# Differential attention: score products of 32 fp32 rows replaced by one split pass over 128-row stacks

## The chip, the cores and the metric

The kernel runs on one core of one Trainium2 chip. The metric is the device time of one execution in microseconds (us). Engines are called PE (TensorE; PEld is its weight load), DVE (VectorE), ACT (ScalarE), POOL (GpSimd) and SP (SyncE, which issues most DMAs). They run their own instruction streams in order and wait for each other by semaphores.

## The reference, cut to what matters

A two-layer backbone over 512 latent tokens and 256 context tokens of width 1024. Each layer normalises the tokens, projects them, and runs four branches (retention, gated linear attention, grouped-query attention, differential attention), whose outputs are projected, gated and summed; then comes a gated MLP. Only differential attention is touched:

```python
def diff_branch(zl, zc, q_norm, k_norm, lam_vecs, subln, layer_idx, rope, need_ctx):
    ...
    ql, kl, vl = prep(zl, True)        # RMS norm of q and k per 32 channels, then rotary (latent tokens only)
    qc, kc, vc = prep(zc, False)
    scale = DIFF_DQK ** -0.5           # DIFF_DQK = 32, 4 heads, 2 maps each
    ...
    ol = blocked_attention(ql, jnp.concatenate([kl, kc], axis=2), jnp.concatenate([v_lat, v_lat], axis=1), scale)
    y_l = combine(ol)                  # o = map0 - lam * map1, then RMS norm
    y_c = combine(blocked_attention(qc, kc, ..., scale)) if need_ctx else None   # layer 0 only
```

So for each of 4 heads and each block of 128 queries there are two score maps, each a product over 32 channels, softmaxed apart and subtracted. Latent queries (4 blocks) see 768 keys, context queries (2 blocks, in layer 0 only) see 256.

## The kernel before, in words

Everything is transposed: channels on the 128 partitions, tokens along the row. All large products are split: an fp32 matrix is kept as a leading part (rounded to the type fp32r, which PE takes in one pass) and a rest (fp32 minus leading part), and a product is three fp32r products: leading x leading, leading x rest, rest x leading (`product`, lines 537 to 539; `token_part`, lines 581 to 583). The weights are split on the fly: SP loads 128x1024 tiles into a ring of four, POOL writes leading part (line 1354) and rest (line 1357) of one half tile after the other (`split`, `split_until`), and PE uses them. Two tiles of split halves fit. POOL therefore runs through the weight tiles in a fixed order, and in program order it does nothing else but the exponents of the gated branch and the rests of the merged sum.

In a layer the branches follow each other on PE. For differential attention the projection of four feature tiles of 128 channels comes first, in the order 2, 3 (keys of heads 0, 1 and of heads 2, 3), 0, 1 (queries of the same heads); then a token projection for the values; then the softmax with its products. Behind each feature tile come its mean squares and, one or two tiles later, the rotation of its channels by a permutation product (`rotate`), which DVE then finishes (`turn`, lines 2130 to 2133). The rotation of tile 0 stands behind the token projection, that of tile 1 behind the transposes of the grouped-query outputs (`turn_outputs`, line 995). The queries' roots don't scale the queries but the scores, by `query_scale`, later.

The outputs of the grouped branch, the first gate tile of the branch (`early_parts`) and then the softmax follow on PE. The softmax waits until the last query tile is rotated. It walks over pairs (query block t, head h), 24 in layer 0 and 16 in layer 1. In each step PE issues the score products of the next head (`scores`, line 827), a share of the gate projection (`among`: 8 gate tiles in layer 0, 10 in layer 1, spread over the steps), and then transposes and value products of the present head (lines 847 and 743). The score products of map 0 and map 1 lie in PSUM banks 0, 1 and 2, 3; each step uses the same banks, so it waits until ACT has taken the exponentials of the step before. DVE finds the maxima (lines 2215, 2216), ACT the exponentials (line 1679), DVE the difference of the maps (lines 2244 to 2246) and every fourth step the normalisation of a query block (lines 2224 to 2235).

A score product before is a plain fp32 product over 32 rows of the rotated tile:

```python
lo, n, qi, ki = 64 * (h % 2) + 32 * m, 32, h // 2, 2 + h // 2
mm = pe.matmul(psum(key)[:, x:y], q[lo:lo + n, qi, t * P:(t + 1) * P], q[lo:lo + n, ki, x:y], ...)
```

Of the kernel before, what the change touches and what calls it, by code (L numbers as in the profile page):

```python
# [245 lines left out]
def bass_hybrid_backbone(nc, A, out, marks):  # L246
# [6 lines left out]
    with ctx:  # L253
# [3 lines left out]
        xT = sb("xT", [P, KT, T])  # L257
        hh_at = nc.sbuf_base
        hh = sb("hh", [P, KT, T], F32R)
        hl = sb("hl", [P, KT, T], F32R)  # L260
# [6 lines left out]
        small = sb("small", [P, sum(w for _, w in SMALL)])  # L267
        rope = sb("rope", [P, 6, LAT])
        dist = sb("dist", [P, 7 * P])
        mask = sb("mask", [P, len(LEVELS), P], U8)  # L270
# [119 lines left out]
        prob = prob.rearrange("p (b m t) -> p b m t", b=2, m=2)  # L390
        pt_s = pt_s.rearrange("p (b t) -> p b t", b=2)

        G = {}
# [119 lines left out]
        def _(pe):  # L513
# [284 lines left out]
            def softmax(l, b):  # L798
# [16 lines left out]

                def scores(t, h):
                    for m in range(maps):
                        for s, c in room(("s", l, b, t, h, m), *((0, 1) if (m if b == "dif" else h % 2) == 0 else (2, 3))):
                            pe.wait_ge(s, c)
                    for x, y in (segs(T) if t < TL else [(LAT, T)]):  # L820
                        for m in range(maps):
                            key = ("s", l, b, t, h, m)
                            if b == "dif":
                                lo, n, qi, ki = 64 * (h % 2) + 32 * m, 32, h // 2, 2 + h // 2
                            else:
                                lo, n, qi, ki = 64 * (h % 2), 64, h // 2, 2 if h // 2 == h % 2 else 3
# [200 lines left out]
            for l in range(DEPTH):  # L1027
# [27 lines left out]
                for b in ORDER:  # L1055
                    nf, nt = len(BR[b]["feat"]), len(BR[b]["tok"])
                    lag = 4 if b == "ret" else 2
                    for j in range(nf + lag):
# [32 lines left out]
                        if b == "dif" and lag <= j < nf + lag - 1:  # L1091
                            rotate(l, b, feature_order(b)[j - lag])
# [232 lines left out]
        def _(pool):  # L1325
# [43 lines left out]
            def rest_of_sum(l, u):  # L1369
# [49 lines left out]
        def _(act):  # L1419
# [197 lines left out]
            def queries_out(l, b, n):  # L1617
# [7 lines left out]
                ins.then_inc(*up("queries", ("turnable", l, b, n)))  # L1625

            def features_out(l, n):

# [25 lines left out]
            def softmax(l, b):  # L1654
# [15 lines left out]
                for n, (t, h) in enumerate(order):  # L1670
# [3 lines left out]
                    for m in range(maps):  # L1674
# [5 lines left out]
                                       bias=nmx[:, c:c + 1],  # L1680
                                       accum_out=rsum[t % 2][:, 4 * m + h:4 * m + h + 1]).then_inc(*up("act_free", ("free", key)))
                    if b == "dif" and n >= 1:
                        transposed(n - 1)
# [193 lines left out]
        def _(dve):  # L1877
# [206 lines left out]
            def prep_tiles(l, b):  # L2084
# [55 lines left out]
                for n in keys if b == "dif" else ():  # L2140
                    if n != keys[0]:
                        turn(n - 1)
                    normalise(n)
                turn(keys[-1])
# [58 lines left out]
            def softmax(l, b):  # L2203
# [81 lines left out]
                for n in range(len(order)):  # L2285
                    t, h = order[n]
                    differ(n)
                    if n + 1 < len(order):
# [270 lines left out]
```

## Time and profile before

| | |
|---|---|
| time, median of 3 runs | 2677.52 us (2672.38 to 2679.13) |
| profiled execution, its own time | 2680.3 us |
| its span, first to last instruction | 2678.5 us |
| busy: PE, PEld, DVE, ACT, POOL | 2558.4, 2120.3, 1361.4, 761.3, 1483.1 us |
| mean granted TensorE clock | 0.986 |
| differential score products | from 708.5 us (layer 0) to 2167.4 us (layer 1) |

Times in the rows are microseconds from the start of the span, durations of single instructions in the views by line are nanoseconds. A row of the order of time gives start, duration, engine, line, operation, what it writes and reads, and in brackets the idle time of its engine before it and what ended that. A matmul's duration includes the way through the array; what PE spends on one is read from the distance of two starts. An fp32 matmul shows as two records, so eight records are the four products of one head.

### The profile page before, as it was taken

How to read it: one execution, taken by the hardware profiler on the slowest of the kernel's cores; microseconds unless marked ns; L12 is line 12 of the kernel's file. 1: busy time of each engine (PE TensorE's matmuls, PEld its weight loads, DVE VectorE, ACT ScalarE, POOL GpSimd, SP SyncE). 2: the span in 40 equal slices, each digit the busy share in tenths (PEclk: the TensorE clock that was granted, in tenths of full speed). 3: DMA queues.
4: the chain of work that ended last, by engine and by line, in shares of the span. 5: the costliest groups of instructions: out<-in, count | busy, mean ns of one | idle time of the engine just before them, and what ended most of it. 6: DMA issues, size and time to landing. Idle time of an engine off the chain costs nothing.

```text
span 2678.5 us, 37843 instructions
## 1 busy us (share of the span) xinstructions
PE 2558.4 (96%) x15408; PEld 2120.3 (79%) x15408; DVE 1361.4 (51%) x1877; ACT 761.3 (28%) x1276; POOL 1483.1 (55%) x1375
## 2 busy tenths in 40 slices
PE   5999999999999999999999999999998998999999
PEld 2788878877777888888878888797877777888777
DVE  3632157643577877555564462327754677521231
ACT  4611333432355511111120123133522454111200
POOL 2443457522423627666669436447834445688886
PEclk8999999999999999999999999999999999999999
DMA  7422312312213833444434462212321237333322
GB/s 270 150 74 95 111 56 70 91 45 93 78 51 98 272 110 111 125 121 117 125 102 118 125 216 77 60 48 79 79 60 48 71 122 220 114 100 95 95 85 81
DMA packets 378210, 285.10 MB, mean 106 GB/s; under 512 B 10309, under 2 KB 338729, under 8 KB 377526
## 3 DMA queue, kind: packets, MB, share of 16 engines
q1 hardware_dynamic: 375744, 279.81, 34.9%
q8 instruction: 123, 2.02, 0.3%
q10 hardware_dynamic: 1686, 2.78, 0.3%
q14 instruction: 49, 0.40, 0.0%
q0 software_dynamic: 608, 0.09, 0.0%
HBM read 253.28 MB, written 29.36 MB: 106 GB/s over the span
## 4 chain that ended last, share of the span: by engine, by line
PE 81%; DVE 9%; POOL 3%; ACT 3%; issue 2%; DMA 1%; ACTq 0%; DVEq 0%; SPq 0%; POOLq 0%
PE ps L537 18%; PE ps L538 17%; PE ps L539 17%; PE ps L1203 3%; PE ps L743 3%; PE ps L581 2%; PE ps L582 2%; PE ps L583 2%; PE ps L827 2%; DVE ffl L2485 2%; POOL w_lo L1357 2%; PE ps L847 2%; PE ps L1152 1%; POOL w_hi L1354 1%; PE ps L955 1%
## 5 line engine op out<-in xcount | busy, mean ns | idle before, releaser
L1354 POOL TENSOR_TENSOR w_hi<-ring,tiny 128x512 fp32r<-128x512 f32 x480 | 535.8, 1116 | 987.4 <-PE ps L539 581.8
L537 PE MATMUL ps<-hh,w_hi 128*128 128x512 f32 (+1 forms) x2320 | 844.4, 364 | 9.9 <-DVE hl L2039 9.0
L1357 POOL TENSOR_TENSOR w_lo<-ring,w_hi 128x512 fp32r<-128x512 f32 (+1 forms) x568 | 798.7, 1409 | 83.5 <-ACT w_hi L1560 45.8
L538 PE MATMUL ps<-hl,w_hi 128*128 128x512 f32 (+1 forms) x2320 | 820.8, 354 | 0.0
L539 PE MATMUL ps<-hh,w_lo 128*128 128x512 f32 (+1 forms) x2320 | 819.9, 353 | 0.0
L537 PEld LDWEIGHTS ps<-hh,w_hi 128*128 128x128 f32 x2320 | 443.1, 191 | 103.4 <-issue 27.1
L539 PEld LDWEIGHTS ps<-hh,w_lo 128*128 128x128 f32 x2320 | 442.9, 191 | 61.8
L538 PEld LDWEIGHTS ps<-hl,w_hi 128*128 128x128 f32 x2320 | 444.0, 191 | 56.1 <-issue 1.0
L1679 ACT ACTIVATE arena<-ps,tiny,vec 128x768 f32<-128x768 f32 (+1 forms) x120 | 108.7, 906 | 188.1 <-DVE tiny L2216 188.0
L1851 ACT ACTIVATE arena<-ps,vec 128x768 f32<-128x768 f32 (+1 forms) x44 | 39.1, 888 | 425.2 <-PE ps L539 425.2
L2494 DVE SCALAR_TENSOR_TENSOR arena<-ps,vec,arena 128x511 f32<-128x511 f32 x66 | 43.6, 661 | 221.3 <-ACT arena L1851 220.5
L537 PE MATMUL ps<-ffh,w_hi 128*128 128x512 f32 x352 | 139.7, 397 | 12.9 <-DVE ffl L2485 11.4
L1962 DVE SCALAR_TENSOR_TENSOR rope<-ring,tiny,rope 128x1024 f32<-128x1024 f32 x84 | 145.4, 1772 | 0.9
L581 PE MATMUL ps<-w_hi,hh 128*128 128x256 f32 x448 | 131.1, 293 | 7.5 <-ACT arena L1613 7.4
L539 PE MATMUL ps<-ffh,w_lo 128*128 128x512 f32 x352 | 137.1, 390 | 0.0
L538 PE MATMUL ps<-ffl,w_hi 128*128 128x512 f32 x352 | 137.1, 390 | 0.0
L582 PE MATMUL ps<-w_lo,hh 128*128 128x256 f32 x448 | 128.6, 287 | 0.0
L583 PE MATMUL ps<-w_hi,hl 128*128 128x256 f32 x448 | 128.5, 287 | 0.0
L2215 DVE TENSOR_REDUCE tiny<-ps 128x1 f32<-128x768 f32 (+1 forms) x120 | 101.3, 845 | 52.7 <-PE ps L811 34.2
L1540 ACT ACTIVATE arena<-ps 128x512 f32<-128x512 f32 (+3 forms) x108 | 59.5, 551 | 192.1 <-PE ps L539 189.7
L581 PEld LDWEIGHTS ps<-w_hi,hh 128*128 128x128 f32 x448 | 88.0, 196 | 13.8 <-ACT arena L1613 8.5
L537 PEld LDWEIGHTS ps<-ffh,w_hi 128*128 128x128 f32 x352 | 66.0, 188 | 36.9 <-DVE ffl L2485 15.8
(271 smaller groups left out, 3820.9 us busy)
## 6 DMA issues: line engine op xcount, KB each, us to landing
ring<-in_w_in SPq DMA_DIRECT2D x118, 512.0 KB, 4.0
ring<-in_w_mod SPq DMA_DIRECT2D x96, 512.0 KB, 3.9
ring<-in_w_up SPq DMA_DIRECT2D x88, 512.0 KB, 4.2
ring<-in_w_down SPq DMA_DIRECT2D x48, 512.0 KB, 3.7
ring<-in_w_out SPq DMA_DIRECT2D x32, 512.0 KB, 3.8
logits<-arena SPq DMA_DIRECT2D x32, 384.0 KB, 2.6
arena<-logits SPq DMA_DIRECT2D x32, 384.0 KB, 4.6
ring<-in_w_down SPq DMA_DIRECT2D x24, 384.0 KB, 3.2
```

The source lines that it names most:

```text
L537: pe.matmul(acc, wh[:, offset + k], hi[:, n, x:y], start=n == 0, stop=False)
L538: pe.matmul(acc, wh[:, offset + k], lo[:, n, x:y], start=False, stop=False)
L539: mm = pe.matmul(acc, wl[:, offset + k], hi[:, n, x:y], start=False, stop=n == whole - 1)
L581: pe.matmul(to, hh[:, n, ts], wh[:, :, k], start=n == 0 and bank_begins, stop=False)
L582: pe.matmul(to, hh[:, n, ts], wl[:, :, k], start=False, stop=False)
L583: mm = pe.matmul(to, hl[:, n, ts], wh[:, :, k], start=False, stop=n == KT - 1 and bank_ends)
L743: mm = pe.matmul(psum(("oT", l, b, t))[64 * s:64 * s + 64, P * c:P * c + P], vt, pt[s][:, m], start=m == key_tiles(t)[0], stop=m == NT - 1)
L1354: pool.tensor_tensor(wh[:, 0:count], w, one[:].unsqueeze(2).to_broadcast([P, count, P]), ALU.mult).then_inc(*up("w_lead", ("lead", key, j)))
L1357: pool.tensor_tensor(wl[:, 0:count], w, wh[:, 0:count].bitcast(F32), ALU.subtract).then_inc(*up("w_split", ("split", key, j)))
L1679: act.activation(prob[:, h % 2, m, lo:T], psum(key)[:, lo:T], ACT.Exp, scale=scale, bias=nmx[:, c:c + 1], accum_out=rsum[t % 2][:, 4 * m + ...
L1962: ins = dve.scalar_tensor_tensor(out=mod_sum[:, s], in0=w, scalar=cs[:, s, k:k + 1], in1=mod_sum[:, s], op0=ALU.mult, op1=ALU.add)
L2215: link(dve.tensor_reduce(nmx[:, c:c + 1], acc[:, lo:T], AX, ALU.max))
```

## The change

Each query block's and key tile's 32 channels of a head and map are stacked to 128 rows: keys as leading part, rest, leading part, rest; queries as leading part, leading part, rest, rest. One fp32r product over the 128 rows then sums all four partial products. Eight stacks (4 heads x 2 maps) are needed for the keys (768 columns), eight for the latent queries (512) and in layer 0 eight for the context queries (256). Each stack has four blocks of 32 rows, each copied from the leading part or the rest of a rotated feature tile.

- ACT makes the leading part of all four tiles (`leading_part`) and copies the leading blocks of key tile 2 and of both query tiles (`leading_blocks`).
- DVE makes the rests (`resting_part`) and copies the rest blocks of the same tiles (`blocks`), in the place where it rotated them.
- POOL copies the sixteen blocks of key tile 3 (`key_blocks`), behind the split of the branch's first gate tile, and waits after each one.
- The blocks of the context queries of tile 0 are copied with that tile, those of tile 1 in step 1 of the softmax, on ACT and DVE.
- PE waits per head for its stacks instead of for the last rotation; the rotation of query tile 0 moves from behind the token projection into its middle.

```diff
+        ROWS_OF = {"k": ("hi", "lo", "hi", "lo"), "q": ("hi", "hi", "lo", "lo"), "c": ("hi", "hi", "lo", "lo")}
+        def part_of(n, which):
+            i = 0 if which == "hi" else 1
+            return o_flat[:, T * i:T * (i + 1)] if n == 1 else pt_s[:, i] if n == 3 else prob[:, i, 1 - i]
+        def stack_blocks(n, kind, which):
+            x, y = {"k": (0, T), "q": (0, LAT), "c": (LAT, T)}[kind]
+            stacks = {"k": K_STACK, "q": Q_STACK, "c": C_STACK}[kind]
+            for h in (2 * (n % 2), 2 * (n % 2) + 1):
+                places = [(i, m) for m in range(2) for i in range(4) if ROWS_OF[kind][i] == which]
+                for i, m in places:
+                    row = 64 * (h % 2) + 32 * m
+                    yield h, stacks[2 * h + m][32 * i:32 * i + 32], part_of(n, which)[row:row + 32, x:y], (i, m) == places[-1]
...
                 def scores(t, h):
+                    if t == 0:
+                        for kind in ("k", "q"):
+                            pe.wait_ge(*at(("stack_hi", l, kind, h)))
+                            pe.wait_ge(*at(("stack_lo", l, kind, h)))
+                    if t == TL:
+                        pe.wait_ge(*at(("stack_hi", l, "c", h)))
+                        pe.wait_ge(*at(("stack_lo", l, "c", h)))
...
-                            mm = pe.matmul(psum(key)[:, x:y], q[lo:lo + n, qi, t * P:(t + 1) * P], q[lo:lo + n, ki, x:y],
+                            key, i = ("s", l, b, t, h, m), 2 * h + m
+                            queries = Q_STACK[i][:, t * P:(t + 1) * P] if t < TL else C_STACK[i][:, (t - TL) * P:(t - TL + 1) * P]
+                            mm = pe.matmul(psum(key)[:, x:y], queries, K_STACK[i][:, x:y],
...
-                pe.wait_ge(*at(("turned", l, b, feature_order(b)[-1])))
                 if b == "gqa":
+                    pe.wait_ge(*at(("turned", l, b, feature_order(b)[-1])))
...
-                                token_projection(l, b, pair, between=(lambda: gate_logits(l, 2)) if b == "gla" else None)
+                                token_projection(l, b, pair, between=(lambda: gate_logits(l, 2)) if b == "gla" else
+                                                 (lambda: rotate(l, "dif", feature_order("dif")[2])) if b == "dif" else None)
...
-                        if b == "dif" and lag <= j < nf + lag - 1:
+                        if b == "dif" and lag <= j < nf:
                             rotate(l, b, feature_order(b)[j - lag])
...
+            def key_blocks(l):
+                pool.wait_ge(*at(("split", ("g", l, gate_tiles(l)["dif"][0]), 1)))
+                for which in ("hi", "lo"):
+                    pool.wait_ge(*at((which, l, 3)))
+                    for n, (h, dst, src, ends) in enumerate(stack_blocks(3, "k", which)):
+                        made = [("moved", l, which, n)] + ([(f"stack_{which}", l, "k", h)] if ends else [])
+                        pool.tensor_copy(dst, src).then_inc(*up("pool_stacks", *made))
+                        pool.wait_ge(*at(("moved", l, which, n)))
...
                 gla_exponents(l)
+                split_until(("g", l, gate_tiles(l)["dif"][0]))
+                key_blocks(l)
                 for u in range(KT):
...
+            def leading_part(l, n):
+                act.wait_ge(*at(("turned", l, "dif", n)))
+                ...
+                act.activation(part_of(n, "hi")[:, 0:w].bitcast(F32R), q[:, n, 0:w], ACT.Copy).then_inc(*up("hi_ready", ("hi", l, n)))
+            def leading_blocks(l, n, kind):
+                act.wait_ge(*at(("hi", l, n)))
+                ...
+                for h, dst, src, ends in stack_blocks(n, kind, "hi"):
+                    ins = act.activation(dst, src, ACT.Copy)
...
                             query_squares(l, b, feature_order(b)[j])
+                        if b == "dif" and j == nf - 1:
+                            leading_part(l, 2)
+                            leading_part(l, 3)
+                            leading_blocks(l, 2, "k")
+                            leading_part(l, 0)
+                            leading_blocks(l, 0, "q")
+                    if b == "dif" and W[l] > LAT:
+                        leading_blocks(l, 0, "c")
                     if b in ("gqa", "dif"):
                         turned_outputs(l, BEFORE[b])
+                    if b == "dif":
+                        leading_part(l, 1)
+                        leading_blocks(l, 1, "q")
...
                 turn(keys[-1])
+                if b == "dif":
+                    resting_part(2)
+                    resting_part(3)
+                    blocks(2, "k", "lo")
                 for n in queries:
                     turn(n)
+                    if b == "dif":
+                        resting_part(n)
+                        blocks(n, "q", "lo")
+                        if n == 0 and W[l] > LAT:
+                            blocks(0, "c", "lo")
```

## Rows read from the trace of the kernel before

**Rows 1.** The page, busy time, share of the span and instructions of each engine.
```profile
PE 2558.4 (96%) x15408; PEld 2120.3 (79%) x15408; DVE 1361.4 (51%) x1877; ACT 761.3 (28%) x1276; POOL 1483.1 (55%) x1375
```
**Rows 2.** One line, the score products: ns min/median/max, first and last start, forms.
```profile
L827 PE MATMUL ps<-arena x288: 374/464/1056, 708.5 to 2167.4; 32*128 32x256 f32 x80, 32*128 32x512 f32 x64
```
**Rows 3.** Windows, PE: length, busy us (count), granted clock, DMA share, GB/s.
```profile
679.89:697.43 17.54, 17.54 (x147) 1.00 0.42 107
721.56:726.73 5.17, 3.84 (x27) 1.00 0.01 2
726.73:733.52 6.79, 6.79 (x50) 0.75 0.01 2
...
2154.38:2160.93 6.55, 6.55 (x51) 1.00 0.40 121
```
**Rows 4.** Order of time on PE, layer 0: split-pass products, one head's scores.
```profile
703.62 0.40 PE L537 MATMUL ps<-hh,w_hi 128*128 128x512 f32 x1
703.85 0.39 PE L538 MATMUL ps<-hl,w_hi 128*128 128x512 f32 x1
...
726.73 1.56 PE L827 MATMUL ps<-arena 32*128 32x512 f32 x8 [1.33 <-ACT arena L1679]
728.22 0.39 PE L537 MATMUL ps<-hh,w_hi 128*128 128x256 f32 x1
```
**Rows 5.** Order of time on DVE, one softmax step of layer 0.
```profile
726.69 0.16 DVE L2244 RECIPROCAL tiny<-tiny 128x1 f32<-128x1 f32 x1 [1.22 <-ACT arena L1679]
...
727.33 1.02 DVE L2246 SCALAR_TENSOR_TENSOR arena<-arena,tiny 128x768 f32<-128x768 f32 x1
728.29 0.96 DVE L2215 TENSOR_REDUCE tiny<-ps 128x1 f32<-128x768 f32 x1
...
731.83 0.16 DVE L2244 RECIPROCAL tiny<-tiny 128x1 f32<-128x1 f32 x1 [1.22 <-ACT arena L1679]
```
**Rows 6.** Order of time on DVE, layer 0: a rotation's last add, the first maximum.
```profile
681.30 1.67 DVE L2133 TENSOR_TENSOR arena<-arena 128x512 f32<-128x512 f32 x1
...
710.16 0.96 DVE L2215 TENSOR_REDUCE tiny<-ps 128x1 f32<-128x768 f32 x1 [1.69 <-PE ps L827]
```
**Rows 7.** Single lines, prices: ns min/median/max, first and last start, forms.
```profile
L1793 ACT ACTIVATE arena<-arena x2: 844/845/846, 534.1 to 1936.9; 64x768 f32<-64x768 f32 x2
L1730 ACT ACTIVATE arena<-arena x70: 618/632/636, 358.3 to 1897.0; 128x512 f32<-128x512 f32 x70
L1917 DVE TENSOR_SCALAR arena<-arena,tiny x6: 749/752/754, 23.5 to 26.9; 128x1024 f32<-128x1024 f32 x6
L1329 POOL MEMSET cs_wide<- x1: 331/331/331, 10.8 to 10.8; 128x256 f32 x1
L1330 POOL MEMSET tiny<- x1: 118/118/118, 11.0 to 11.0; 128x1 f32 x1
L1354 POOL TENSOR_TENSOR w_hi<-ring,tiny x480: 612/1042/2037, 51.8 to 2659.1; 128x512 fp32r<-128x512 f32 x160
L1399 POOL TENSOR_TENSOR arena<-arena x140: 394/412/877, 356.8 to 1896.0; 128x128 f32<-128x128 f32 x140
```
**Rows 8.** Order of time on POOL: last operation of the first gate tile, both layers.
```profile
698.63 1.27 POOL L1357 TENSOR_TENSOR w_lo<-ring,w_hi 128x512 fp32r<-128x512 f32 x1
...
2060.68 1.28 POOL L1357 TENSOR_TENSOR w_lo<-ring,w_hi 128x512 fp32r<-128x512 f32 x1
```
**Rows 9.** Order of time on PE: starts of the softmax, both layers.
```profile
715.23 0.50 PE L537 MATMUL ps<-hh,w_hi 128*128 128x512 f32 x1
...
2069.67 2.68 PE L827 MATMUL ps<-arena 32*128 32x512 f32 x8 [3.58 <-issue]
...
2078.79 0.50 PE L537 MATMUL ps<-hh,w_hi 128*128 128x512 f32 x1
```
**Rows 10.** Windows, PE, columns as in rows 3: behind two idle times.
```profile
2070.00:2077.00 7.00, 7.00 (x20) 0.51 0.12 36
728.00:732.00 4.00, 4.00 (x22) 0.57 0.01 4
```

More of the change, by code:

```diff
@@ L258, in bass_hybrid_backbone @@
         hh_at = nc.sbuf_base
+        xT_at = hh_at - 4 * KT * T
         hh = sb("hh", [P, KT, T], F32R)
@@ L391, in bass_hybrid_backbone @@
         pt_s = pt_s.rearrange("p (b t) -> p b t", b=2)
+        k_low = nc.alloc_sbuf_tensor_at("k_low", [P, 2, T], F32R, offset=arena_at + 4 * 7 * T)
+        k_high = nc.alloc_sbuf_tensor_at("k_high", [P, 4, T], F32R, offset=arena_at + 4 * 19 * T)
+        k_x = nc.alloc_sbuf_tensor_at("k_x", [P, 2, T], F32R, offset=xT_at + 4 * 6 * T)
+        q_rope = nc.alloc_sbuf_tensor_at("q_rope", [P, 4, LAT], F32R, offset=rope_at)
+        q_low = nc.alloc_sbuf_tensor_at("q_low", [P, 4, LAT], F32R, offset=arena_at)
+        c_low = nc.alloc_sbuf_tensor_at("c_low", [P, 7, CTX], F32R, offset=arena_at + 4 * 4 * LAT)
+        c_high = nc.alloc_sbuf_tensor_at("c_high", [P, CTX], F32R, offset=arena_at + 4 * (scratch0 + 6 * 256 + 2 * T - CTX))
+        K_STACK = [k_high[:, i] for i in range(4)] + [k_low[:, i] for i in range(2)] + [k_x[:, i] for i in range(2)]
+        Q_STACK = [q_rope[:, i] for i in range(4)] + [q_low[:, i] for i in range(4)]
+        C_STACK = [c_low[:, i] for i in range(7)] + [c_high[:]]
+        ROWS_OF = {"k": ("hi", "lo", "hi", "lo"), "q": ("hi", "hi", "lo", "lo"), "c": ("hi", "hi", "lo", "lo")}
[10 more added lines that the diff above has]
+                    yield h, stacks[2 * h + m][32 * i:32 * i + 32], part_of(n, which)[row:row + 32, x:y], (i, m) == places[-1]
         G = {}
@@ L816, in scores @@
                 def scores(t, h):
+                    if t == 0:
[5 more added lines that the diff above has]
+                        pe.wait_ge(*at(("stack_lo", l, "c", h)))
                     for m in range(maps):
-                        for s, c in room(("s", l, b, t, h, m), *((0, 1) if (m if b == "dif" else h % 2) == 0 else (2, 3))):
+                        for s, c in room(("s", l, b, t, h, m), *((0, 1) if m == 0 else (2, 3))):
                             pe.wait_ge(s, c)
@@ L1625, in queries_out @@
                 ins.then_inc(*up("queries", ("turnable", l, b, n)))
+            def leading_part(l, n):
+                act.wait_ge(*at(("turned", l, "dif", n)))
+                if n == feature_order("dif")[0]:
+                    act.wait_ge(*at(("pv", l, "gqa", NQ[l] - 1, 3)))
+                if n == 0:
+                    act.wait_ge(*at(("lo", l, 2)))
+                    act.wait_ge(*at(("stack_hi", l, "k", 1)))
+                w = W[l] if is_q("dif", n) else T
+                act.activation(part_of(n, "hi")[:, 0:w].bitcast(F32R), q[:, n, 0:w], ACT.Copy).then_inc(*up("hi_ready", ("hi", l, n)))
+            def leading_blocks(l, n, kind):
+                act.wait_ge(*at(("hi", l, n)))
+                if n == 1:
+                    act.wait_ge(*at(("lo", l, n)))
+                for h, dst, src, ends in stack_blocks(n, kind, "hi"):
+                    ins = act.activation(dst, src, ACT.Copy)
+                    if ends:
+                        ins.then_inc(*up("act_stacks", ("stack_hi", l, kind, h)))
             def features_out(l, n):
@@ L1681, in softmax @@
                                        accum_out=rsum[t % 2][:, 4 * m + h:4 * m + h + 1]).then_inc(*up("act_free", ("free", key)))
+                    if b == "dif" and n == 1 and W[l] > LAT:
+                        leading_blocks(l, 1, "c")
                     if b == "dif" and n >= 1:
@@ L2143, in prep_tiles, with resting_part, blocks @@
                     normalise(n)
+                def resting_part(n):
+                    w = W[l] if is_q(b, n) else T
+                    dve.wait_ge(*at(("hi", l, n)))
+                    if n == 0:
+                        dve.wait_ge(*at(("stack_lo", l, "k", 1)))
+                    step(dve.tensor_tensor(part_of(n, "lo")[:, 0:w].bitcast(F32R), q[:, n, 0:w], part_of(n, "hi")[:, 0:w], ALU.subtract),
+                         "lo_ready", ("lo", l, n))
+                def blocks(n, kind, which):
+                    for h, dst, src, ends in stack_blocks(n, kind, which):
+                        ins = dve.tensor_copy(dst, src)
+                        if ends:
+                            ins.then_inc(*up("dve_stacks", (f"stack_{which}", l, kind, h)))
                 turn(keys[-1])
+                if b == "dif":
+                    resting_part(2)
+                    resting_part(3)
+                    blocks(2, "k", "lo")
                 for n in queries:
                     turn(n)
+                    if b == "dif":
[3 more added lines that the diff above has]
+                            blocks(0, "c", "lo")
                     key, r = ("qkn", l, b, n), query_roots(l, b, n)
@@ L2286, in softmax @@
                     t, h = order[n]
+                    if n == 1 and W[l] > LAT:
+                        for h1, dst, src, ends in stack_blocks(1, "c", "lo"):
+                            ins = dve.tensor_copy(dst, src)
+                            if ends:
+                                ins.then_inc(*up("dve_stacks", ("stack_lo", l, "c", h1)))
                     differ(n)
```

6 lines of the change are left out of this document (1 added, 5 removed).

## The prediction

> **What bounds the kernel now.** I read the page's busy times first, then the line of the score products, then windows over single steps of the differential softmax (from one pair of score products to the next), then DVE, ACT, POOL and PE in order of time around the start of that softmax, and last the prices of single operations.
>
> PE is busy 96% of the span [rows 1], so PE work taken away should be time. But the stage that is touched has a second limit. One head's step there is: two score products on PE, two maxima on DVE, two exponentials on ACT, the difference of the maps on DVE, transposes on PE. The next head's scores use the same PSUM banks, so they wait for the exponentials. In the step at 721.56 us PE was busy 3.84 of 5.17 us, in the one at 726.73 it was 6.79 of 6.79 [rows 3]: some steps are PE's, some are the loop's. The loop by itself [rows 5]: the reciprocal of one head at 726.69, the difference at 727.33 (1.02 long), the next maximum at 728.29 right behind it, the next reciprocal at 731.83. That is 5.14 us. The scores (726.73 to 728.22) lie beside the difference, so 5.14 is a floor that shorter scores don't move. Step lengths by the starts of the score pairs (31; two steps of layer 0 and one of layer 1 stand in [rows 3]): layer 0 from 713.74: 7.82, 5.17, 6.79, 5.17, 6.56, 5.17, 9.54, 5.18, 5.24, 5.17, 6.56, 5.17, 6.68, 5.33, 6.99; layer 1 from 2077.30: 7.82, 5.17, 6.57, 5.18, 6.56, 5.32, 7.80, 5.14, 9.29, 5.35, 7.74, 5.14, 6.55, 5.32.
>
> **The score products.** There are 144, 64 with 512 columns and 80 with 256 [rows 2]: 32 heads of two maps, and 8 context heads with the 256 alone. A full head holds PE from 726.73 to 728.22, 1.49 us; split-pass products of 128 rows follow each other at 0.23 us for 512 columns [rows 4], so 0.12 for 256. A head becomes 2 x 0.23 + 2 x 0.12 = 0.70 us and saves 0.79; for a context head I take 0.35.
>
> 1.49 us is little for four fp32 products: at four passes each, one after the other, they would take 4 x 0.70 = 2.8. The two maps, which lie in different row groups, already run side by side. The Trainium skill has this as a rule (TensorE: Matmul & The Clock Gate, Part 3: Packing small matmuls): products in different row groups run at once, and a 32-row product alone takes as long as one of 128 rows. The 1.49 agrees. Who leaves the rule out books 2.1 us a head, 67 in all, where 25 are to be had.
>
> 32 heads at 0.79 and 8 at 0.35 would be 28 us, but only steps that are PE's own can give it. Not counting the first, four in each layer are well over the floor without idle time on PE (layer 0: 6.79, 6.56, 9.54, 6.68; layer 1: 6.57, 6.56, 9.29, 6.55): 8 x 0.79 = 6.3. The steps of 5.14 to 5.18 give nothing. Those of 5.24 to 5.35, and those that wait for the normalisation of a query tile, I put at 1.7 together, five context steps at 1.8, the last head of each layer at 1.2 together. Sum **11 us**; bounds 6 (the eight alone) and 24 (were the loop no floor).
>
> **What is added, and where it lies.** Per layer: four leading parts on ACT, four rests on DVE, and 64 blocks of 32 rows (16 for each of four tiles; 768 columns for keys, 512 for queries), in layer 0 another 32 of 256 columns. ACT's SBUF copies cost 0.845 us at 768 and 0.63 at 512 [rows 7], so 0.42 at 256. DVE's one-input operation costs 0.752 at 1024 [rows 7]; with a fixed part I take 0.6, 0.47 and 0.33; should a copy run as slowly as DVE's PSUM reads (0.96 at 768 [rows 6]), 0.96, 0.69 and 0.42.
>
> Key tile 2 and query tile 0 are prepared beside the token projection, 17.54 us in which PE has no idle time [rows 3], with the rotation of tile 0 now in its middle. Key tile 3 is rotated at 683.0 [rows 6]. ACT: its leading part to 683.9, eight blocks to 690.6. DVE: two rests, eight blocks to 690, rotation of query tile 0 to 692.6. ACT: leading part to 693.4, eight blocks to 698.4. The projection ends at 698.5 (1.05 later than before; the rotation is saved behind it), so the values leave PSUM almost in time, and PE's transposes of the grouped outputs start about 1 us late; at the upper prices 3.
>
> Query tile 1 has no such cover. Its rotation starts at 704.3 and ends near 707, for an add takes 1.67 us beside POOL [rows 6] where the shortest takes 0.69. Leading part 0.8, rest 1.2, eight DVE blocks 3.8 to 5.6, root scales 1: DVE reaches the first maximum at 714 to 716, not at 710.16 [rows 6]. The first exponentials end at 717 to 719 and with them the second pair of scores starts, 4 to 6 late. In layer 1, where PE stood idle 3.58 us for this rotation [rows 9], the same sum gives 2077.5 to 2080 against 2077.30. The context blocks of tile 1 (3.3 us on ACT) come while PE is in the first gate part and cost nothing; without that cover 2.5.
>
> **POOL decides the start.** Its 16 blocks stand between the split of the first gate tile and that of the second, which PE needs right behind the second pair of scores (715.23 and 2078.79 [rows 9]). Behind the blocks are queued all later splits, and behind that gate part, in PE's order, the transposes of head 0. The split of the first tile ends at 699.9 and 2062.0 [rows 8], with the 1.05 at 701 and 2063. No copy on POOL is in the trace. From below: a memset takes 0.331 at 256 columns and 0.118 at one [rows 7], 0.75 for 768. From above: the two-input operation takes 1.042 at 512 and 0.412 at 128 [rows 7], 1.46 for 768. With 0.08 between operations 16 blocks take 13.3 to 24.6 us. One operand fewer puts the copy nearer the memset, DVE's copies beside it stretch it: I take 18. The Trainium skill (GPSIMD Engine Reference, 4.1 Engine selection) calls one-input work there roughly line rate; an estimate from its clock on that page is 0.64 us a block, 10 in all, and the sum would then be that of the first rival. No row shows such a copy.
>
> With 18 the blocks end at 719 and 2081 and both halves of the next split (2.4 to the first) let PE go on at 721.4 and 2083.4: the gate part starts **6.2 late in layer 0 and 4.6 in layer 1**. Bounds: 2.8 and 0 (DVE's delay alone), 12.8 and 11.2.
>
> PE stands idle there for 6 to 10 us, one pair of scores apart. In layer 1, after 3.58 us of idle time, the granted clock was 0.51 for 7 us, the 1.2 GHz level [rows 9, 10]: the pair took 2.68 instead of 1.56, the 12 products behind it 5.1 instead of 2.8, together 3.4 lost. I add 3.4 in each layer, **6.8**; bounds 0 and 8. Shorter scores also leave longer gaps in the steps at 5.17; behind an idle time of 1.33 us the clock was 0.57 from 728 to 732 [rows 4, 10], 1.7 lost. Two more such dips: **3.4**, bounds 0 and 8.
>
> **Sum.** 6.2 + 4.6 + 6.8 + 3.4 - 11 = +10.0 us. The profiled execution took 2680.3 us (span 2678.5), 2.8 above the median of 2677.5; so 2690.3 for it, 2687.5 by the median. I say **2688**.
>
> **Rivals.**
> - *The start is covered* (0.29). POOL's copy takes 0.75 and DVE's blocks their low price: start 2.8 and 0, one cold stretch 3.4, one dip 1.7, gain 11: -3, about 2674. For it speaks the memset; against it how POOL and DVE slow each other.
> - *The whole saving lands on PE* (0.17): the loop is no floor. For it: the score pair at 726.73 ends at 728.22, 0.07 ahead of the maximum, so either could have released it. Against: 727.33 + 1.02 is 728.35. Its place is the steps at 5.14 to 5.18; the gain is 24, the start with its cold stretches 11: -13, 2664. It decides once those steps fall under 4.6.
> - *POOL copies at the two-input price* (0.12): 12.8 + 11.2 + 6.8 + 3.4 - 11 = +23, 2701. For it: nearly all of POOL's work in the trace runs at that price.
> - That the products do not shrink would need split-pass products slower than those of [rows 4]; no chance of its own.
>
> **How the numbers follow.** Forecast 0.42, its own range 2680 to 2697. The bound of 0.3%, 8 us, is about what a measurement of this kernel can tell from no change. Three tenths of the forecast lie under it, and seven of the first rival lie within it, two above, one below. Slower: 0.42 x 0.7 + 0.12 + 0.29 x 0.2 = 0.47. Faster: 0.17 x 0.9 + 0.29 x 0.1 = 0.18. Same: the remaining 0.35. The range 2666 to 2703 holds the forecast, the first rival and the nearer halves of the other two.
>
> **What would show it.** Right: some 0.7 us a head on the scores' line; POOL's copies ahead of the second gate tile's split at about 1.1 us each; PE's first gate product behind the second pair of scores waiting on POOL, the clock at 0.5 behind it; steps of 5.1 to 5.2 unchanged. Wrong: copies at 0.75 and no wait of PE on POOL; the first maximum under 3 us late; steps under 5.0 us.

## The result, and the profile after

The changed kernel is a little slower: 2681.69 us (median of 20 runs, 2677.28 to 2687.90) against 2676.94 us for the kernel before beside it (20 runs, 2667.85 to 2682.91). The ratio is 1.0023, 95% interval 1.0014 to 1.0032, so 6.2 us more, 3.7 to 8.6. The profiled executions are the closest pair that the two kernels have: 2680.49 us (span 2678.7) and 2680.3 us (span 2678.5). They are read for where time goes inside the softmax, not for the difference of the whole.

PE has 31 us less to do [rows 1], and one head's scores are short. First the page's line of busy times, then the line of the scores for two of the key stacks (columns as in [rows 2]), then PE in order of time in a quiet step, where the next product starts 0.77 us after the scores (1.49 before, [rows 4]).

```profile
PE 2527.4 (94%) x15264; PEld 2115.5 (79%) x15264; DVE 1405.5 (52%) x1949; ACT 806.4 (30%) x1348; POOL 1508.8 (56%) x1407
```
```profile
L860 PE MATMUL ps<-k_low,q_low x32: 274/336/504, 736.3 to 2166.2; 128*128 128x512 f32 x16, 128*128 128x256 f32 x16
L860 PE MATMUL ps<-k_x,q_low x32: 274/339/472, 740.7 to 2171.2; 128*128 128x512 f32 x16, 128*128 128x256 f32 x16
```
```profile
777.70 0.93 PE L860 MATMUL ps<-k_low,q_low 128*128 128x512 f32 x4 [0.44 <-ACT arena L1746]
778.47 0.28 PE L566 MATMUL ps<-hh,w_hi 128*128 128x256 f32 x1
```

The start of each softmax pays for it. PE in order of time at the second pair of scores, layers 0 and 1 (the same place as in [rows 9]): PE stands idle 11.80 and 10.29 us for ACT's first exponentials; the first gate product follows at once, so it waits for no split of POOL; and both run at the 1.2 GHz level (second fence, windows with columns as in [rows 3]: granted clock 0.50 behind the idle time).

```profile
726.67 1.62 PE L860 MATMUL ps<-k_high,q_rope 128*128 128x512 f32 x4 [11.80 <-ACT arena L1746]
728.09 0.63 PE L566 MATMUL ps<-hh,w_hi 128*128 128x512 f32 x1
...
2086.56 1.62 PE L860 MATMUL ps<-k_high,q_rope 128*128 128x512 f32 x4 [10.29 <-ACT arena L1746]
2087.98 0.63 PE L566 MATMUL ps<-hh,w_hi 128*128 128x512 f32 x1
```
```profile
728.10:732.10 4.00, 4.00 (x11) 0.50 0.68 189
2088.00:2091.00 3.00, 3.00 (x9) 0.50 0.77 202
```

ACT waited for DVE's first maximum, and DVE was late by its own copies. DVE in order of time, layer 0 (start, us, operation, count; [rows 6] has the maximum of before at 710.16): eight copies of 32x512 take 3.48 us for query tile 0 and 8.56 for tile 1; eight of half that size take 7.09.

```profile
695.03 3.48 DVE L2237 CAST q_rope<-arena 32x512 fp32r<-32x512 f32 x8
698.53 7.09 DVE L2237 CAST c_low<-arena 32x256 fp32r<-32x256 f32 x8
...
707.33 0.69 DVE L2210 TENSOR_TENSOR arena<-ps,rope 128x512 f32<-128x512 f32 x1
...
712.34 8.56 DVE L2237 CAST q_low<-arena 32x512 fp32r<-32x512 f32 x8
...
723.09 0.96 DVE L2321 TENSOR_REDUCE tiny<-ps 128x1 f32<-128x768 f32 x1
```

POOL at that time is in its sixteen copies (701.12 to 716.87) and then in its splits:

```profile
701.12 3.47 POOL L1416 CAST k_low<-arena 32x768 fp32r<-32x768 f32 x4
704.66 3.49 POOL L1416 CAST k_x<-arena 32x768 fp32r<-32x768 f32 x4
708.21 4.79 POOL L1416 CAST k_low<-arena 32x768 fp32r<-32x768 f32 x4
713.06 3.81 POOL L1416 CAST k_x<-arena 32x768 fp32r<-32x768 f32 x4
716.94 1.09 POOL L1388 TENSOR_TENSOR w_hi<-ring,tiny 128x512 fp32r<-128x512 f32 x1
```

Single lines show the same over both layers (ns min/median/max; 16 instructions each): the same 32x512 copy is 0.420 us at its median where POOL is idle, 0.952 us where POOL works, and no tile 1 copy is under 0.934.

```profile
L2237 DVE CAST q_rope<-arena x16: 417/420/423, 695.0 to 2063.2; 32x512 fp32r<-32x512 f32 x16
L2237 DVE CAST q_low<-arena x16: 934/952/1390, 712.3 to 2081.1; 32x512 fp32r<-32x512 f32 x16
```

Against the same place in the kernel before, the second pair of scores of layer 0 comes 12.93 us late (726.67 against 713.74) and the third 14.69 (736.25 against 721.56). By the last scores of layer 0 the delay is down to 5.00 (839.83 against 834.83). In layer 1 it is 9.26 at the second pair and 4.31 at the last (2170.56 against 2166.25), but 3.89 of both is carried over from layer 0: the last scores of layer 1's grouped branch start at 1995.25, before at 1991.36. Layer 1's own start costs 5.4 us and its loop gives 5.0 of them back, so that nearly all of the delay that is left is layer 0's. Start paid, loop gave back: that is the form that the forecast had, with another engine in the middle and other sizes.

### The profile page after: what moved, and what is told of

Read it like the earlier page. It is cut to its first block, busy times and chain, and to the rows that moved or that the text cites. A ratio compares the mean times of both kernels' runs of the same rounds, so it can differ in the third digit from the quotient of the medians.

```text
span 2678.7 us, 37766 instructions
## 1 busy us (share of the span) xinstructions
PE 2527.4 (94%) x15264; PEld 2115.5 (79%) x15264; DVE 1405.5 (52%) x1949; ACT 806.4 (30%) x1348; POOL 1508.8 (56%) x1407
## 4 chain that ended last, share of the span: by engine, by line
PE 75%; DVE 14%; ACT 5%; POOL 3%; issue 2%; DMA 1%; ACTq 0%; DVEq 0%; SPq 0%; POOLq 0%
PE ps L566 17%; PE ps L567 16%; PE ps L568 16%; PE ps L1237 3%; PE ps L772 3%; PE ps L610 2%; DVE ffl L2596 2%; PE ps L611 2%; PE ps L612 2%; POOL w_lo L1391 2%; ACT arena L1746 2%; PE ps L880 1%; PE ps L1186 1%; POOL w_hi L1388 1%; PE ps L988 1%
```

## Experiments

Step below means the time from one pair of score products to the next, and a quiet step is one of 5.14 to 5.35 us in the kernel before. Theory A: DVE's block copies, slowed by whatever POOL does beside them, carry the start, and the scores gain in nearly every step. Rivals: POOL's late split is what PE waits for (the forecast); the number of copies or the handshakes with ACT carry the start; a copy costs the same wherever it stands. All ratios are to the kernel before, run beside each.

**1. The gain alone.** All copies stay, the scores are fp32 products of 32 rows again (of one 32-row block of each stack, so they are not the reference's scores).

```diff
-                            mm = pe.matmul(psum(key)[:, x:y], queries, K_STACK[i][:, x:y],
+                            lo = 64 * (h % 2) + 32 * m
+                            mm = pe.matmul(psum(key)[:, x:y], queries[lo:lo + 32].bitcast(F32), K_STACK[i][lo:lo + 32, x:y].bitcast(F32),
```


> All copies of the change stay, the scores alone are again fp32 products of 32 rows (row groups side by side, 1.49 us a head); they read one 32-row block of each stack, so the scores are not the reference's. It prices the gain by itself. Theory A (the split pass gains in nearly every step of the loop; from the traces of before and after 7.8 us in the first layer behind the second step and 6.6 in the second, 14.4 in all): 14 us above the changed kernel, about 2696 us, start as late as there (first maximum near 723 and 2083), quiet steps back at 5.14 to 5.17. Rival B (the step as forecast: the loop of maximum, exponential and difference is a floor, only eight steps gain, 11 us): 2692 to 2693. Rival C (the scores were hidden, the change is all cost): within 3 us of the changed kernel, 2679 to 2685.

Ratio 1.0092 (1.0077 to 1.0108), 24.6 us above the kernel before and, from the difference of the two ratios, 18.5 above the changed kernel, some 5 us either way. That is more than B's 11; whether it is more than A's 14 the runs alone can't tell. Step by step (starts of the score pairs, this run minus the changed kernel) the sum is 17.7: 3.6 in the two first steps, 8.8 in the 11 long ones, 5.7 in the 16 quiet ones (5.14 to 5.35 here; 4.44 to 4.97 there but for two; the sixteenth is the one of 6.79 in the kernel before), -0.4 in the context steps. A's count had left out the first steps. The quiet step itself, DVE in this run: the difference ends at 754.85 + 1.02 = 755.87, and the maximum starts at 756.01, when the scores (next fence, PE) end. In the kernel before it is the same in all 15 quiet steps: the first maximum starts within 0.03 us of the end of the scores, as in the line of that kernel in the third fence (its scores end at 721.56 + 1.56).

```profile
754.85 1.02 DVE L2353 SCALAR_TENSOR_TENSOR arena<-arena,tiny 128x768 f32<-128x768 f32 x1
756.01 0.96 DVE L2322 TENSOR_REDUCE tiny<-ps 128x1 f32<-128x768 f32 x1
```
```profile
754.44 1.56 PE L861 MATMUL ps<-k_high,q_rope 32*128 32x512 f32 x8
```
```profile
723.15 0.96 DVE L2215 TENSOR_REDUCE tiny<-ps 128x1 f32<-128x768 f32 x1 [2.19 <-PE ps L827]
```

In the changed kernel the maximum follows the difference without a gap (747.34 behind 746.40 + 1.02), and the loop takes 4.92 (745.95 to 750.87):

```profile
745.95 0.17 DVE L2350 RECIPROCAL tiny<-tiny 128x1 f32<-128x1 f32 x1 [1.22 <-ACT arena L1746]
746.15 0.22 DVE L2351 SCALAR_TENSOR_TENSOR tiny<-tiny 128x1 f32<-128x1 f32 x1
746.40 1.02 DVE L2352 SCALAR_TENSOR_TENSOR arena<-arena,tiny 128x768 f32<-128x768 f32 x1
747.34 0.95 DVE L2321 TENSOR_REDUCE tiny<-ps 128x1 f32<-128x768 f32 x1
...
750.87 0.16 DVE L2350 RECIPROCAL tiny<-tiny 128x1 f32<-128x1 f32 x1 [1.22 <-ACT arena L1746]
```

**2. Without POOL's copies.** Heads 2 and 3 read key tile 2's stacks in their place.

```diff
-                key_blocks(l)
...
-                            mm = pe.matmul(psum(key)[:, x:y], queries, K_STACK[i][:, x:y],
+                            mm = pe.matmul(psum(key)[:, x:y], queries, K_STACK[i % 4][:, x:y],
```


> GpSimd's sixteen copies are left out, heads 2 and 3 read the stacks of key tile 2, so their scores are not the reference's. Theory A (VectorE's copies are stretched by GpSimd's at the same time and carry the start): the eight tile 1 copies of VectorE take 3.5 us instead of 8.56 and 7.71, the eight context copies 2.4 instead of 7.09; first maximum near 713.5 in the first layer (723.09) and near 2079 in the second (2082.98); then ScalarE's tile 1 copies and table load are the last, second pair of scores near 722 (726.67) and 2083 (2086.56); 6 to 10 us below the changed kernel, 2672 to 2676. Rival B (the number of copies on VectorE carries it, GpSimd does not disturb them): copies at 1.0 us as before, first maximum moves by under 1 us, time within 2 us of the changed kernel. Rival C (GpSimd's late split is what TensorE waits for): the first gate product comes earlier, VectorE's copies keep their time, 4 to 8 us below.

Ratio 1.0013 (1.0005 to 1.0022), 2.7 us below the changed kernel, which the intervals can't tell from none: a miss for A's numbers. Tile 1's copies took 5.19 and 6.20 us and the context copies 7.77; the first maximum moved to 720.04 only. But POOL was not quiet. Its splits had moved into the free place (701.25 to 708.4, then from 716.06 to 721.1), and the copies slowed down just there: the line's minimum and median are those of the quiet copy, its maximum 1397 ns.

```profile
L2236 DVE CAST q_low<-arena x16: 418/421/1397, 713.7 to 2079.3; 32x512 fp32r<-32x512 f32 x16
L2236 DVE CAST c_low<-arena x8: 285/1033/1335, 701.1 to 708.6; 32x256 fp32r<-32x256 f32 x8
```

**3. The second gate tile's split ahead of the copies.**

```diff
-                split_until(("g", l, gate_tiles(l)["dif"][0]))
+                for g in gate_tiles(l)["dif"][:2]:
+                    split_until(("g", l, g))
                 key_blocks(l)
...
+                        if n <= 2:
+                            act.wait_ge(*at(("stack_hi" if n == 1 else "stack_lo", l, "k", 3)))
                         transposed(n - 1)
```


> GpSimd splits the second gate tile ahead of the key copies instead of behind them (ScalarE's two first copies of turned weights wait for the key copies by name). The step of the forecast (the late split costs 6.2 and 4.6 us): 6 to 11 us below the changed kernel, 2671 to 2676. Theory A (VectorE's chain to the first maximum carries the start, the split is not waited for): no gain; the key copies come some 5 us later, now beside all of VectorE's tile 1 copies, second pair of scores at the same place or up to 2 us later, time within 2 us of the changed kernel or up to 3 above.

Ratio 1.0022 (1.0013 to 1.0032), the changed kernel's own. PE's second pair still waits for ACT, 12.06 us in layer 1. With DVE's copies in front of it, the forecast's late split is not the price.

```profile
2082.92 1.62 PE L860 MATMUL ps<-k_high,q_rope 128*128 128x512 f32 x4 [12.06 <-ACT arena L1747]
2084.34 0.63 PE L566 MATMUL ps<-hh,w_hi 128*128 128x512 f32 x1
```

**4. Query tile 1's copies behind steps 0 and 1.** On DVE (and likewise on ACT behind the exponentials):

```diff
+                    if n < 2:
+                        for h1, dst, src, ends in stack_blocks(1, "q", "lo"):
+                            if h1 == 2 + n:
+                                ins = dve.tensor_copy(dst, src)
+                                ...
                     differ(n)
```


> Query tile 1's copies (heads 2 and 3) leave the path to the first maximum: VectorE copies head 2 behind the maxima of step 0 and head 3 behind those of step 1, ScalarE likewise behind the exponentials of steps 0 and 1. Theory A (VectorE's chain carries the start): first maximum near 714.5 in the first layer (723.09) and 2076 in the second (2082.98), second pair of scores 7 to 9 us earlier; each of steps 0 and 1 grows by 2 to 4 us where the copies sit between exponential and difference; 4 to 6 us less in each layer, 2670 to 2674 us. Rival C (GpSimd's splits are what counts): the second pair of scores is early, but its gate products wait for the split until 719.4 and 2079, 0 to 3 us less in each layer, 2676 to 2682. Rival D (the copies cost the same wherever they stand, since VectorE is on the chain of each step): the start gains 8, the steps give 8 back, within 2 us of the changed kernel.

Ratio 1.0014 (1.0004 to 1.0023), 2.4 us below the changed kernel, which the intervals can't tell from none. The first maximum came even before the time that A gave (713.66 and 2072.07) and the second pair at 717.24, 9.43 earlier. The steps then took it back, but in two ways. In layer 0 the step behind the third pair took 10.75 us (4.45 in the changed kernel): twelve context and query copies, 725.52 to 732.50, stand ahead of the difference for which PE waits. That is D. In layer 1 the step behind the second pair took 14.87 us (8.95), and 5.13 of it is PE's wait for POOL's split: that is C, and the wait of the forecast (in layer 0 it was 0.81). Of tile 1's sixteen copies twelve took 0.95 to 1.49 us beside POOL, four 0.42 to 0.52.

```profile
734.15 1.51 PE L880 MATMUL ps<-small,arena 128*128 128x128 f32 x6 [5.03 <-DVE arena L2356]
...
2081.72 0.77 PE L566 MATMUL ps<-hh,w_hi 128*128 128x512 f32 x1 [5.13 <-POOL w_lo L1391]
```

**5. POOL held idle.** As experiment 2, and POOL's next splits wait for the first maximum.

```diff
-                key_blocks(l)
+                pool.wait_ge(*at(("max", l, "dif", 0, 0, 1)))
```


> As the run without GpSimd's copies (heads 2 and 3 read key tile 2's stacks, so their scores are not the reference's), and GpSimd's next splits wait for the second map's first maximum: GpSimd stands idle from about 701 and 2066 to the first maximum. It measures what stretches VectorE's copies. Theory A (any work of GpSimd beside them does, splits as well as copies): all of VectorE's copies at the quiet price, tile 1's eight 3.5 us (8.56 and 7.71 in the changed kernel, 5.19 and 6.20 without GpSimd's copies alone), the context tile's eight 2.4 us (7.09, 7.77); first maximum near 714 and 2076, the exponential then waits for ScalarE's tile 1 copies and table load until about 718 and 2077; the gate products of step 1 wait for the late split, 2.4 us behind the first maximum. Time 2671 to 2678. Rival B (it is the destination or TensorE's reads that stretch them): tile 1's copies stay at 5 us or more.

Ratio 0.9997 (0.9987 to 1.0006), 7 us below the changed kernel. Tile 1's copies fell to the quiet price in both layers, with not one slow copy among 16:

```profile
L2237 DVE CAST q_rope<-arena x16: 417/420/424, 695.0 to 2056.3; 32x512 fp32r<-32x512 f32 x16
L2237 DVE CAST q_low<-arena x16: 418/420/424, 710.0 to 2069.6; 32x512 fp32r<-32x512 f32 x16
```

From the start of tile 1's rotation to the first maximum DVE needs 8.26 and 8.07 us here (705.98 to 714.24, 2062.66 to 2070.73) against 15.76 and 13.35 in the changed kernel (707.33 to 723.09, 2069.63 to 2082.98): 7.5 and 5.3 us of the start are POOL's work beside DVE's. The context copies still took 4.20 us, the first ones beside the split that ends at 701.0. So work of POOL of either kind slows DVE's copies, and neither their destination nor PE's reads do. It is not the whole of the start: the second pair came at 719.30, 7.37 earlier than in the changed kernel and still 5.6 later than before, and now PE waited (4.41 us) for exponentials that stood behind ACT's own copies and table load.

**6. Half of DVE's copies.** Stacks of 96 rows without the product of the two rests.

```diff
-ROWS_OF = {"k": ("hi", "lo", "hi", "lo"), "q": ("hi", "hi", "lo", "lo"), "c": ("hi", "hi", "lo", "lo")}
+ROWS_OF = {"k": ("hi", "lo", "hi"), "q": ("hi", "hi", "lo"), "c": ("hi", "hi", "lo")}
...
```


> The stacks have 96 rows instead of 128: leading times leading, rest times leading, leading times rest; the product of the two rests (a fourth of the blocks) is left out, so VectorE makes half of its copies (4 of 512 columns for a query tile), GpSimd 12 instead of 16, ScalarE as many as before. Theory A (VectorE's copies, stretched from 0.43 to 1.07 us by whatever GpSimd does beside them, carry the start): first maximum near 717 in the first layer (723.09 with 128 rows) and near 2079 in the second (2082.98), then ScalarE's eight tile 1 copies and table load are late by a little; 3 to 6 us less in each layer, 2671 to 2675 us, about the time before the change or a little below. Rival E (the number of copies does not matter, the handshakes between ScalarE and VectorE do): within 2 us of the changed kernel, 2680 to 2684. Either way the scores take 0.70 us a head and the quiet steps 4.45 and 4.92, since 96 rows take TensorE as long as 128.

Ratio 0.9989 (0.9979 to 1.0000): 9.1 us below the changed kernel; the 2.9 below the kernel before can't be told from none. First maximum at 717.33; second pair of scores at 720.98, 5.7 earlier. A.

**7. 96 rows, and tile 1's copies late.** The edits of experiments 4 and 6 together.

> 96 rows, and query tile 1's copies behind the maxima and exponentials of steps 0 and 1 (2 on VectorE and 4 on ScalarE in each). Theory A: first maximum near 713 and 2072 (before the change 710.16 and 2072.38); in each of steps 0 and 1 two copies of VectorE (1 to 2.2 us beside GpSimd) stand in the 1.2 to 2.5 us that it waits for the exponentials, so the steps give nothing back; start 2 to 4 us behind the kernel before instead of 9 to 13, the loop's gain of some 17 us stays: 2663 to 2668, 9 to 14 us below the kernel before. Rival D (a copy costs the same wherever it stands): as the 96 rows alone, 2671 to 2675.

Ratio 0.9985 (0.9972 to 0.9997), no better than the 96 rows alone: a miss. The first maximum was early as forecast (713.04, 2068.94), but new waits came behind it. In layer 0 the step behind the third pair took 9.39 us: ACT in order of time has query copies, context copies and two reads of PSUM ahead of the next exponential, which starts 7.4 us after the last one ended. In layer 1 PE waited 3.21 us for the exponentials and 0.80 for POOL's split. ACT, layer 0:

```profile
723.32 2.55 ACT L1692 ACTIVATE q_low<-arena 32x512 fp32r<-32x512 f32 x4
725.90 2.56 ACT L1692 ACTIVATE c_low<-arena 32x256 fp32r<-32x256 f32 x6
728.47 0.84 ACT L1692 ACTIVATE c_high<-arena 32x256 fp32r<-32x256 f32 x2
729.33 0.81 ACT L1734 ACTIVATE arena<-ps 128x768 f32<-128x768 f32 x1
730.04 0.59 ACT L1586 ACTIVATE arena<-ps 128x512 f32<-128x512 f32 x1
730.66 0.99 ACT L1748 ACTIVATE arena<-ps,tiny,vec 128x768 f32<-128x768 f32 x1
```

**8. The query scales in DVE's wait.** Experiment 7 with the three scale operations ahead of the rest.

```diff
                     turn(n)
+                    key, r = ("qkn", l, b, n), query_roots(l, b, n)
+                    ...
                     if b == "dif":
                         resting_part(n)
...
-                    key, r = ("qkn", l, b, n), query_roots(l, b, n)
-                    ...
```


> The kernel with 96 rows and late tile 1 copies, and the three small query scale operations of each tile ahead of the rest (VectorE waits there 0.8 to 1.0 us for ScalarE's leading part) instead of behind the copies. Theory A: the wait is filled, the first maximum comes 0.6 to 1.0 us earlier in each layer, 1 to 2 us below the run without it. Rival: the scales wait for the roots or for ScalarE's output there, no gain, within 1 us.

Ratio 0.9981 (0.9972 to 0.9990). The first maximum is 0.5 and 1.2 us earlier; the time, 1.1 us less than experiment 7, can't be told from none.

**9. The context copies spread over steps 2 and 3.** On both engines:

```diff
-                    if n == 1 and W[l] > LAT:
+                    if n in (2, 3) and W[l] > LAT:
                         for h1, dst, src, ends in stack_blocks(1, "c", "lo"):
+                            if h1 != n:
+                                continue
...
```


> The kernel with 96 rows, late tile 1 copies and scales first, and in the first layer the second context tile's copies behind steps 2 and 3 (heads 2 and 3) instead of all behind step 1, where ScalarE's queue of query copies, context copies and the turned weights made the step 9.42 us. Theory A (that queue sets the step): it falls to 6 to 7 us, steps 2 and 3 grow by under 1 us together; 2 to 3 us less, 2665 to 2668. Rival: VectorE or the gate products set that step, nothing changes, 2668 to 2670.

Ratio 0.9966 (0.9953 to 0.9978): 9.1 us below the kernel before and 4.0 below experiment 8, where the intervals allow some 4 for noise. The step itself fell from 9.42 to 5.98 us, and PE's wait for ACT ahead of the transposes in it from 4.40 to 0.97. The edit moves DVE's copies too, so that ACT's queue set the step is read from that wait and from the rows of experiment 7.

**10. And the split ahead of the copies.** Experiment 9 with the edit of experiment 3.

> The same, and the second gate tile's split ahead of GpSimd's key copies. With the start short, TensorE's first gate product of the second layer waited 0.8 us for this split (2074.25). Theory A: that wait goes, up to 1 us less in the second layer, if the key copies, now some 5 us later, are still there at step 2 (their end near 717 and 2076, needed at 723 and 2081); the copies then lie beside VectorE's tile 1 work as much as before: 0 to 1.5 us below the run without it, 2664 to 2668. The step of the forecast (the split is worth 4.6 to 6.2 us in a layer) would give 2655 to 2660.

Ratio 0.9959 (0.9945 to 0.9972), 11.0 us below the kernel before, 17 below the changed kernel: the best of these. Beside experiment 9 it is 1.9 us, within the intervals. The traces do differ: with the start short, PE's first gate product of layer 1 waited 1.60 us for POOL's split in experiment 9 (first fence), and the step took 10.23 us at a granted clock of 0.83; here it took 6.85, at full clock (second fence, windows over that step in layers 0 and 1). The six steps behind it, 4.7 us longer together, took that back.

```profile
2067.30 0.93 PE L860 MATMUL ps<-k_high,q_rope 96*128 96x512 f32 x4 [2.50 <-ACT arena L1748]
2069.83 0.76 PE L566 MATMUL ps<-hh,w_hi 128*128 128x512 f32 x1 [1.60 <-POOL w_lo L1391]
```
```profile
715.95:722.75 6.80, 6.80 (x34) 1.00 0.15 59
2064.31:2071.16 6.85, 6.85 (x34) 1.00 0.11 42
```

## Why the prediction was right or wrong

The sum was +10.0 us, measured are +6.2 (3.7 to 8.6). The form held: a start that costs more than the loop gives. But the gain was forecast too small, and the cause named for the start was not the one that decided: that the total came out near is in part luck.

- **A head's scores, 0.70 us.** Right: 0.77 from the scores to the next product, against 1.49.
- **The gain, 11.** Mis-sized: 17.7 by the steps, 18.5 by the runs. The step that failed is "5.14 is a floor that shorter scores don't move". The step of [rows 5] was not a typical one: its small operation between reciprocal and difference took 0.41 us beside a split of POOL that ended at 727.28; the median of its 40 is 0.22. That delay let the difference end 0.06 behind the scores and so hid that the scores release the maximum, as they do in all 15 quiet steps. DVE's own loop is 4.92, and where DVE has finished its difference early the step falls to 4.45. The list has 29 steps, not 31, and the count of four long ones in layer 0 leaves one out: two have 6.56 without idle time on PE (0.8 more). The rival "the whole saving lands on PE" had named the sign (the scores end 0.07 ahead of the maximum), but it was not that either: its steps were to fall under 4.6 and 24 us to come, and nine of the 16 quiet ones stop at 4.92 to 4.97. The 1.8 from the context steps did not come (-0.4).
- **"POOL decides the start", 6.2 and 4.6.** This step failed: the wait that ends last is another. At neither start did PE wait for POOL, and moving the split ahead changed nothing (experiment 3). DVE decided: its first maximum came at 723.09 in layer 0, not at 714 to 716, and in layer 1 at 2082.98, 10.6 later than before, of which 3.9 is carried over. Eight DVE blocks were taken at 3.8 to 5.6 us; they took 8.56 and 7.71. That POOL and DVE slow each other stood in the text, for the adds of a rotation and for POOL's price, but not in the price of DVE's blocks. The forecast's wait does exist, behind the larger one: once tile 1's copies are out of the way, PE waits 5.13 us for the split in layer 1 (experiment 4), 0.80 in experiment 7 and 1.60 in experiment 9.
- **POOL's copies, 18 us for 16.** Good: 15.8 in each layer, 0.82 and 0.90 at the medians of its two destinations, at most 1.44 beside DVE.
- **ACT's and DVE's prices where POOL is idle.** For 768, 512 and 256 columns: ACT 0.842, 0.630 and 0.414, as taken; DVE 0.55, 0.42 and 0.29, a little below the lower end.
- **Cold clock, 6.8.** The clock fell as said, to 0.50 in both layers. It costs 2.7 in layer 0 (the pair 1.62 for 0.93, the products behind it 7.75 for 5.74) and 2.1 in layer 1 (7.12). But layer 1's first pair, which ran cold before (2.68, [rows 9]), now takes 0.85, with the products behind it at a granted clock of 1.00: it no longer waits for tile 1's rotation. The forecast did not see that the wait it described would go from there, and the 3.4 us lost there before with it.
- **Dips in the loop, 3.4.** None beyond those of before. From the third pair to the last scores the granted clock is 0.98 and 1.00 (first fence), in the kernel before 0.97 and 1.00 and with the old scores 0.98 and 1.00 (experiment 1, second fence):

```profile
736.25:839.83 103.58, 92.75 (x682) 0.98 0.17 49
...
2095.51:2170.56 75.05, 68.75 (x451) 1.00 0.27 76
```
```profile
738.86:850.54 111.68, 107.00 (x749) 0.98 0.15 46
2106.28:2187.37 81.09, 79.01 (x501) 1.00 0.24 69
```

All costs together were forecast at 21.0; with the old scores the kernel is 24.6 (20.6 to 28.9) above the kernel before, so the size of the costs held within the interval, while their make-up did not. The gain was short by some 7 us, the costs by some 4, and in the sum these stand against each other: that it is off by 4 us only is luck.

The wait that decided is one that the Trainium skill describes (SBUF — State Buffer, Who interferes with whom): VectorE's copies in SBUF can take a second pair of ports that it shares with GpSimd, whoever issues first holds it for the whole instruction, and the other waits. The traces agree: a 32x512 copy is 0.420 us where GpSimd is idle, and in the changed kernel 0.934 to 1.390 us beside GpSimd's splits and copies. GpSimd's own copies take 0.82 us with VectorE idle, 0.90 beside VectorE's copies of tile 1 and 1.17 beside its adds with two inputs in SBUF. That the ports are the reason no run here shows by itself. The same section says that ScalarE never waits; its copies for tile 1 took 0.627 to 0.632 us beside all of that.

## What to carry to other kernels

When work is given to an idle GpSimd to relieve VectorE, look at what VectorE does at the same time: here its SBUF copies cost more than double beside GpSimd's copies and splits, so the offload lengthened the chain that it was to shorten. Price a copy on VectorE twice, with GpSimd idle and busy, and put fewer copies on the way to the first result (experiment 6); ScalarE's copies kept their price, but giving it more of them was not tried. When a wait is taken off the path, look for the one behind it: here it was GpSimd's split, then ScalarE's queue. Before a loop length is called a floor, compare several steps of it: a step that a neighbour has stretched can hide which engine released the next.

## What the runs showed of the hardware

- Two-input operations of DVE are slowed beside POOL too: the last add of tile 1's rotation took 0.69 us with POOL held idle (experiment 5) and 1.20 in the changed kernel; the maxima over 768 columns in PSUM took 0.94 to 0.96 in both.
- ACT's 32-row copies cost what copies of more rows and the same length do: 0.842 against 0.845 us of a 64-row one at 768 columns, 0.630 against 0.632 of a 128-row one at 512 [rows 7]. POOL's 32x768 copy, 0.82 us at the lower median, lies near the bound from its memset (0.75), far from that of its two-input operation (1.46).
- A product of 96 rows takes PE as long as one of 128: the four of a head show as 0.93 to 0.94 us at full clock in both.
